# Low halves of the first layer's weights: an adding DMA in place of a VectorE subtraction

## The reference, cut to what matters

```
m = silu(c) @ w_mod + b_mod                  # shift, scale, gate
h = rmsnorm(x, norm_g) * (1 + scale) + shift
z, bg, cg, xh = split(h @ w_in, 4)           # w_in: 1024 x 8192
y = cg * xh
y = yp[:-2]*w0 + yp[1:-1]*w1 + yp[2:]*w2     # three taps along the tokens, yp: y padded
x = x + gate * ((bg * y * silu(z)) @ w_out)
```

## Time and profile before

| what | value |
|---|---|
| median of 3 runs | 862.37 us (862.34 to 863.28) |
| the profiled execution, its span | 860.2 us |
| TensorE busy | 839.6 us (98%) |
| VectorE busy | 509.2 us (59%) |
| ScalarE busy | 271.7 us (32%) |
| GpSimd busy | 27.7 us (3%) |
| moved by DMA | 106.23 MB, mean 124 GB/s |

### The profile page before, as it was taken

How to read it: one execution, slowest core, us unless ns; L and a number is a source line. 1 busy time by engine, 2 the same in 40 slices (tenths; PEclk the granted TensorE clock), 3 DMA queues, 4 the chain that set the end, 5 groups by cost and what they waited for, 6 DMA issues and landing times.

```text
span 860.2 us, 11815 instructions
## 1 busy us (share of the span) xinstructions
PE 839.6 (98%) x4018; PEld 705.3 (82%) x4018; DVE 509.2 (59%) x824; ACT 271.7 (32%) x334; POOL 27.7 (3%) x28
## 2 busy tenths in 40 slices
PE   5899999999999999999999999999999999999997
PEld 5678888888888888888889888888888888888896
DVE  5999655555556556564333675558666766753334
ACT  3343222222212222222222662234443444432210
POOL 2510000000000000000000100000000000000000
PEclk9899999999999999999999999999999999999999
DMA  7677525353444444442221233223222222223202
GB/s 266 226 262 252 195 98 176 116 171 122 157 135 141 134 140 146 146 146 98 98 97 50 99 100 111 89 69 120 74 98 79 91 98 98 97 75 98 73 1 98
DMA packets 30849, 106.23 MB, mean 124 GB/s; under 512 B 3312, under 2 KB 5488, under 8 KB 30832
## 3 DMA queue, kind: packets, MB, share of 16 engines
q1 hardware_dynamic: 30544, 104.95, 36.4%
q10 hardware_dynamic: 288, 1.05, 0.4%
HBM read 103.89 MB, written 2.10 MB: 123 GB/s over the span
## 4 chain that ended last, share of the span: by engine, by line
PE 93%; DVE 4%; DMA 1%; issue 0%; ACT 0%; SPq 0%; DVEq 0%
PE pp L437 26%; PE pp L439 26%; PE pp L438 26%; PE pp L635 3%; PE pp L636 3%; PE pp L637 3%; DVE acc L760 3%; PE p_aux L688 1%; DMA x<-in_xt 1%; PE p_aux L459 1%; PE pp L521 1%; DVE w_lo L740 1%; PE p_aux L691 0%; PE p_aux L481 0%; DVE x L1178 0%
## 5 line engine op out<-in xcount | busy, mean ns | idle before, releaser
L740 DVE TENSOR_TENSOR w_lo<-raw,w_hi 128x1024 fp32r<-128x1024 f32 x144 | 175.8, 1222 | 208.0 <-ACT w_hi L268 207.8
L268 ACT ACTIVATE w_hi<-raw 128x1024 fp32r<-128x1024 f32 x144 | 152.6, 1061 | 447.3 <-PE pp L439 382.9
L437 PE MATMUL pp<-h_hi,w_hi 128*128 128x512 f32 x720 | 282.4, 392 | 0.0
L439 PE MATMUL pp<-h_hi,w_lo 128*128 128x512 f32 x720 | 280.4, 389 | 0.0
L438 PE MATMUL pp<-h_lo,w_hi 128*128 128x512 f32 x720 | 280.2, 389 | 0.0
L439 PEld LDWEIGHTS pp<-h_hi,w_lo 128*128 128x128 f32 x720 | 135.2, 188 | 28.8
L438 PEld LDWEIGHTS pp<-h_lo,w_hi 128*128 128x128 f32 x720 | 135.3, 188 | 27.4
L437 PEld LDWEIGHTS pp<-h_hi,w_hi 128*128 128x128 f32 x720 | 135.2, 188 | 27.2
L437 PE MATMUL pp<-y_hi,w_hi 128*128 128x512 f32 (+1 forms) x320 | 111.5, 348 | 0.0
L439 PE MATMUL pp<-y_hi,w_lo 128*128 128x512 f32 (+1 forms) x320 | 110.9, 347 | 0.0
L438 PE MATMUL pp<-y_lo,w_hi 128*128 128x512 f32 (+1 forms) x320 | 110.9, 347 | 0.0
(11 more groups left out here) (114 smaller groups left out, 669.3 us busy)
## 6 DMA issues: line engine op xcount, KB each, us to landing
raw<-in_stream SPq DMA_DIRECT2D x192, 512.0 KB, 3.3
x<-in_xt SPq DMA_DIRECT2D x4, 512.0 KB, 6.7
out_t<-x SPq DMA_DIRECT2D x8, 256.0 KB, 2.3
rs_bc<-in_wst ACTq DMA_DIRECT2D x1, 512.0 KB, 4.6
bs_bc<-in_bs ACTq DMA_DIRECT2D x1, 512.0 KB, 5.4
cols<-in_cols SPq DMA_DIRECT2D x1, 80.0 KB, 1.9
```

The lines of the kernel that those rows point to most:

```text
L268: act.activation(w_hi[:, slot[0], :], raw[:, slot[1], :], ACT.Copy).then_inc(hi_cut, 1)
L437: pe.matmul(out, hi, rhs_hi(kt), start=first and n == 0, stop=False)
L439: mm = pe.matmul(out, lo, rhs_hi(kt), start=False, stop=last and n == len(kts) - 1)
L740: dve.tensor_tensor(w_lo[:, slot[0], :], raw[:, slot[1], :], f32(w_hi[:, slot[0], :]), ALU.subtract).then_inc(consumed, 1)
```

## The change

In passes 1 to 7 ScalarE follows each high half by a second activation that writes the negated high half, as the float32r copy of the raw slot times -1, into the `w_lo` slot. GpSimd waits for it, counts in `lo_begun`, and issues a DMA that adds the raw slot to it in place. Where VectorE subtracted, it now waits for that DMA (`lo_in`, one semaphore for each slot) and fills two columns of the tile `term` (unused in this loop) with zeros; this fill counts in `consumed`. Pair 0 and all other loops keep the subtraction.

```diff
@@ -169,6 +169,8 @@
         dve_step = sem("dve_step")
+        neg_cut, lo_begun = sem("neg_cut"), sem("lo_begun")
+        lo_in = [sem(f"lo_in{j}") for j in range(RING)]
@@ -253,6 +255,13 @@
                 if k in (0, 2):
                     pool.wait_ge(stat_sum, k + 1)
                     pool.memset(ssum[:, :], 0.0).then_inc(sq_added, 1)
+                if k == 0:
+                    with pool.Fori(1, PAIRS) as i:
+                        for s in range(8):
+                            pool.wait_ge(neg_cut, 8 * i + (s + 1 - 8))
+                            pool.sem_inc(lo_begun, 1)
+                            pool.dma_start(w_lo[:, (s + LEAD) % 4, :].bitcast(F32), raw[:, (A_Q0 + A_W_AT[s]) % 4, :],
+                                           accum_op=ALU.add).then_inc(lo_in[(s + LEAD) % 4], 16)
@@ -330,6 +339,7 @@
                 for s in range(8):
                     q = A_Q0 + A_W_AT[s]
                     cut_hi(8 * i + (s + LEAD), ((s + LEAD) % 4, q % 4), 48 * i + q_round(q))
+                    act.activation(w_lo[:, (s + LEAD) % 4, :], raw[:, q % 4, :], ACT.Copy, scale=-1.0).then_inc(neg_cut, 1)
@@ -916,8 +926,8 @@
                     if first:
                         cut_lo_start(s + LEAD)
                     else:
-                        q = A_Q0 + A_W_AT[s]
-                        cut_lo(8 * i + (s + LEAD + 1), ((s + LEAD) % 4, q % 4))
+                        dve.wait_ge(lo_in[(s + LEAD) % 4], 32 * i + (16 * (s // 4 + 1) - 32))
+                        dve.memset(term[:, 0, 2 * s:2 * s + 2], 0.0).then_inc(consumed, 1)
```

## The result

The changed kernel took 865.21 us (864.33 to 867.21, 6 runs) against 863.15 (862.34 to 863.83, 6 runs) in the same session: ratio 1.0027, 95% interval 1.0015 to 1.0039. It is slower by 2 us, 0.3%. The forecast was 862.4 within 861 to 930, with no change at 0.57 and slower at 0.41, so the time is inside the range, but on the less likely side of the 0.2% line. In two further sessions the ratio was 1.0020 (1.0008 to 1.0032) and 1.0031 (1.0014 to 1.0048). The profiled execution has a span of 863.8 us, where it was 860.2.

What follows compares the result with a forecast made beforehand. TensorE, busy for all 312.00 us of the loop, was taken as the bound. Removed and added work lay under its cover, so all path terms were 0: span 860.2, median 862.4 us, range 861 to 930.

Steps and rivals of the forecast that it cites:

- rival A: Loop: the chain of raw slots becomes the bound if L passes 9.0 us; 898 us at L = 11; chance 0.26.
- the sum: Loop path: low half whole after 8.4 us of 16.3 allowed, three links 36.3 of 44.5; all terms 0, median 862.4.
- What bounds the kernel, and removed and added work: Loop, 80 to 392 us: TensorE alone; 68 us of subtractions removed, 59 us of negated copies added, worth 0.
- L: Loop: time from negated half to landed sum, GpSimd issue plus adding transfer, 6.3 us (3.3 to about 13).
- The load in a link: Loop: raw load within one link (load, two scalar instructions, transfer; 12.1 us), taken as 3.7 us.
- A pass's DMA time: Loop: 12 loads at 1.56 us and 8 sums at 3.1 take 43.5 of a pass's 44.5 us.
- Who waits for what: Loop: TensorE waits for weights (7.9 us spare) and PSUM pairs; modulation sums merely stand behind vector engine waits; cost 0.
- the ring: Loop: four raw slots serving twelve loads a pass; three links through steps 0, 3, 5, 0 leave 8.2 us spare.
- My sign of being wrong: Loop: matmuls waiting for the fills, or high halves waiting for loads at steps 3 and 0.
- the chain that I laid: Loop: raw slot through steps 3, 5 and next pass's 0; step 5's high half 1.2 us late, weights in time.
- B: Loop: the DMA engines become full, 23.8 us more a pass, 1029 us; chance 0.15.
- C: Loop: fills wait for the sum, so the vector engine is less busy but later; time and chance within the forecast's.

Runs made afterwards that it cites:

- bystander run: Kernel before, subtractions kept, plus 56 adding DMAs of the same size into an idle buffer, waited for by GpSimd alone: 863.17 us, ratio 1.0002.
- repaired for both limits and the end: Changed kernel with negated copy before high half, fourth modulation slot summed ahead of taps, 16 idle GpSimd semaphore counts: 862.53 us, ratio 0.9997.

## Why the prediction was right and wrong

The time lies in the range, but the range was wide for rival A's sake, and the sum had no term for what was lost. Of the 2 us none was in the forecast: it came from a path that was not listed, and from the end.

- *What bounds the kernel, and removed and added work:* right. VectorE lost 63 us net and ScalarE gained 52, beside a busy TensorE, and neither shows in the time; the fill took 0.06 us where I had bounded it by 0.16, the negated copy 1.04 for 1.06, the issue on GpSimd 0.87 for 1.0.
- *L:* mis-sized by little. I had 6.3 us from negated half to sum; measured are 0.6 us of handing over and 6.4 from issue to landing, 7.0. The second read at 1.56 us was right in kind: without the addition the landing is 1.9 us shorter. The rule of the Trainium skill (Collectives: The Full Stack, section on the bandwidth ceiling), that a reducing transfer pays for its second read, agrees with that. Fixed cost plus bytes by the Trainium skill (DMA: Bandwidth & Descriptors, section on the anatomy of one DMA on the GpSimd path) gave estimates of 3.2 and 4.4 us, where these runs have 4.4 and 6.3 beside the loads.
- *The load in a link at 3.7 us:* too small, the most mis-sized term of the sum. I took it from a loop whose DMA engines were 0.44 busy and did not raise it for the traffic that I added in the next sentence. Beside the adding DMAs it is 5.0 to 5.2. A link is then 5.2 + 2.0 + 0.6 + 6.4 = 14.2 us and three are 42.6, not 36.3. Step 5 comes up to 7 us late and not 1.2.
- *A pass's DMA time:* I had 12 x 1.56 + 8 x 3.1 = 43.5 us of 44.5; measured 12 x 1.55 + 8 x 2.84 = 41.3, 0.93, and the window says 0.91. TensorE's blocks kept their beat beside nearly full engines, but loads lengthened and scattered (3.2 to 7.3 us in the loop, before 3.0 to 4.7), as they did in the bystander run (3.2 to 7.8).
- *Who waits for what:* here is the step that was missing. I listed TensorE's waits for the weights and for the two PSUM pairs, and put the modulation sums down only as things behind VectorE's waits. TensorE's column matmuls wait for the same counter, for m3. With my own durations the chain from step 1 would have been 8.4 + 2.0 + 3.7 + 8.4 + 3.6 + 2.0 = 28.1 us of 33.1, spare enough in the mean. Measured in the seven passes, the means are 9.1 to step 1's fill, 7.7 for m1 and the load, 10.0 to step 4's fill and 5.5 for taps and m3: 32.3 of 32.7, so it is late whenever a transfer is.
- *Sizes as means:* a mean L below 9 was my condition for no loss. Landings from 4.5 to 9.1 us meet a fixed beat. In the three profiles of the changed kernel the columns have 0.4, 0.9 and 1.0 us to spare in the mean and are still late in five passes of 21, by up to 1.7 us; the kernel's 28 executions take from 862.2 to 870.4 us.
- *The end of the kernel:* the 0.6 us that go with the fetch were nowhere in the sum.
- *Rivals:* A was the one that came nearest, in its first traces: the ring drifted, without a stall in most profiles. My sign of being wrong, high halves that wait for loads at steps 0 and 3, came (31 waits on loads; the high halves of steps 0 and 3 up to 3 us late, of step 2 up to 5.8), and the ring still did not become the bound, since the weights had their spare time behind it. Step 2 wasn't on the chain that I laid: its slot passes through m3 and m0, which are counted late as well. Of the rule weighed under A, that GpSimd writes no descriptors while VectorE is in a two-port mode (Trainium skill, SBUF — State Buffer, who interferes with whom): issues took 0.85 to 1.05 us throughout, and the three that ran beside a tensor-scalar pair 0.90, so no lock of the size of such a pair shows in them; whether these instructions run in that mode, and what it may do to landings, wasn't tried. B did not come. C holds: VectorE waits 190.5 us for the sums.

## What to carry to other kernels

Before work is moved from an engine to a DMA, list every waiter on the counter that now counts later, TensorE's small matmuls among them, and walk each chain from slot to slot once around the loop. Price the transfers with the traffic that the change adds: engines going from 0.44 to 0.91 busy made the old loads 1.5 us slower. And keep a margin of a landing's spread, not of its mean; repaired for both limits and the end, the adding DMA is as fast as the subtraction (0.9997), and no faster, since TensorE was the bound. And when a loss of 1 us is hunted, set stage beside stage, not span beside span: over these profiles the loop began within 2.4 us of time, and for the changed kernel alone within 1.8.

## What the runs showed of the hardware

- An adding DMA of 512 KB within SBUF, issued by GpSimd, landed in 6.3 us (4.5 to 9.1) and a copying one in 4.4 (2.8 to 6.6), with GpSimd busy for 0.86 and 0.53 us.
- HBM loads of 512 KB went from 3.7 to 5.0 us beside such transfers that nobody waited for.
- Ten profiles with an 8 KB instruction fetch (queue 14) during the last output's transfer end 0.6 to 0.7 us later than the four without; sixteen idle counts in GpSimd's program took both away.
- The mean granted clock in 10 to 45 us was 0.90, 0.85 or 0.80, and differed between executions of one kernel. In the profiles with 0.90 the column matmuls just ahead of the loop stand at 78.6 to 79.1 us, in those with 0.80 at 80.4 to 81.0.
